# Weight loads of 1 MB instead of 512 KB in a decoder block on one Trainium2 core

## What is computed

```
h = rmsnorm(x, g_pre_mix)
nq, nkv, ngate, rq, rk, rv, rg, mq, bg = split(h @ w_in)            # 2048 x 12824
y_a = nsa_attention(nq, nkv, sigmoid(ngate), cmp_w1_k, cmp_w1_v, ...)  # 8 heads
y_b = retention(rq, rk, rv) * silu(rg)                              # 4 heads
y_c = memory_attention(mq, rmsnorm(mem) @ w_mem_kv)                 # 4 heads, 256 memory rows
merged = sum over 3 branches of sigmoid(bg[b]) * (y_b @ w_br[b])
x = x + rmsnorm(merged @ w_o, g_post_mix)
u = causal_dwconv(rmsnorm(x) @ w_up)                                # 2048 x 11264
x = x + rmsnorm((gelu(u_gate) * u_val) @ w_down, g_post_ffn)        # 5632 x 2048
```

## Time and profile before

| | us |
|---|---|
| median of 3 runs | 1735.86 (1735.41 to 1736.28) |
| the profiled execution, its own time | 1736.51 |
| span of that execution, first to last instruction | 1734.0 |
| mean granted TensorE clock | 0.998 of 2.4 GHz |
| PE busy | 1708.6 (99% of the span) |
| DVE, ACT, POOL busy | 1090.6, 817.0, 44.5 |
| moved by DMA | 327.77 MB, 189 GB/s in the mean |

### The profile page before, as it was taken

One profiled execution on the slowest core, in us unless ns is written; L12 is line 12 of the kernel. 1 busy time (PEld: TensorE's weight loads), 2 busy tenths in 40 slices (PEclk: granted clock), 3 DMA queues, 4 the chain that ended last, 5 costly groups with the idle time before them and its releaser, 6 DMA issues.

```text
span 1734.0 us, 26478 instructions
## 1 busy us (share of the span) xinstructions
PE 1708.6 (99%) x9645; PEld 1500.4 (87%) x9645; DVE 1090.6 (63%) x1430; ACT 817.0 (47%) x1111; POOL 44.5 (3%) x50
## 2 busy tenths in 40 slices
PE   6999999999999999999999999999999999999998
PEld 6998999999888888888888888888888888888886
DVE  5645557666566454564565667776676676676677
ACT  5533346444444434434444555454454454454453
POOL 0000000000041000000000000000000000000000
PEclk9999999999999999999999999999999999999999
DMA  8756467545555666666657555655666666656654
GB/s 262 223 184 188 146 194 243 161 131 165 157 189 180 193 196 193 214 197 193 190 179 241 184 171 190 189 192 187 189 194 189 188 193 189 192 187 191 191 184 141
DMA packets 246146, 327.77 MB, mean 189 GB/s; under 512 B 12727, under 2 KB 167464, under 8 KB 245544
## 3 DMA queue, kind: packets, MB, share of 16 engines
q1 hardware_dynamic: 246056, 326.47, 60.4%
HBM read 321.71 MB, written 3.67 MB: 188 GB/s over the span
## 4 chain that ended last, share of the span: by engine, by line
PE 94%; DVE 2%; DMA 2%; issue 1%; ACT 1%; SPq 0%; POOL 0%; POOLq 0%; DVEq 0%; ACTq 0%
PE bank L1347 18%; PE bank L1338 15%; PE bank L1337 15%; PE bank L1339 15%; PE bank L1351 9%; PE bank L1311 4%; PE bank L1313 4%; PE bank L1312 4%; PE bank L1324 1%; PE bank L1326 1%; PE bank L1325 1%; DMA wraw<-in_w_in 1%; DVE wlo L840 1%; PE bank L1647 0%; PE bank L1626 0%
## 5 line engine op out<-in xcount | busy, mean ns | idle before, releaser
L840 DVE TENSOR_TENSOR wlo<-wraw,whi 128x1024 fp32r<-128x1024 f32 x580 | 711.0, 1231 | 470.0 <-ACT whi L564 468.5
L564 ACT ACTIVATE whi<-wraw 128x1024 fp32r<-128x1024 f32 x580 | 613.2, 1060 | 702.0 <-PE bank L1339 390.5
L1347 PE MATMUL bank<-hx,whi 128*128 128x512 f32 x1376 | 344.5, 392 | 0.0
L1347 PEld LDWEIGHTS bank<-hx,whi 128*128 128x128 f32 x1376 | 248.0, 189 | 44.9
L1351 PEld LDWEIGHTS bank<-hx,wlo 128*128 128x128 f32 x1376 | 187.7, 190 | 13.4
L1351 PE MATMUL bank<-hx,wlo 128*128 128x256 f32 x1376 | 191.9, 282 | 0.0
L1337 PE MATMUL bank<-whi,hx 128*128 128x512 f32 x448 | 175.7, 392 | 0.0
L1339 PE MATMUL bank<-whi,hx 128*128 128x512 f32 x448 | 174.4, 389 | 0.0
L1338 PE MATMUL bank<-wlo,hx 128*128 128x512 f32 x448 | 174.3, 389 | 0.0
L1337 PE MATMUL bank<-whi,r_hi 128*128 128x512 f32 x384 | 149.8, 390 | 0.0
L1338 PE MATMUL bank<-wlo,r_hi 128*128 128x512 f32 x384 | 149.5, 389 | 0.0
(11 more groups left out here) (264 smaller groups left out, 2136.8 us busy)
## 6 DMA issues: line engine op xcount, KB each, us to landing
wraw<-in_w_in SPq DMA_DIRECT2D x200, 512.0 KB, 3.6
wraw<-in_w_up SPq DMA_DIRECT2D x176, 512.0 KB, 4.4
wraw<-in_w_down SPq DMA_DIRECT2D x88, 512.0 KB, 4.2
wraw<-in_w_mem_kv SPq DMA_DIRECT2D x32, 512.0 KB, 3.8
wraw<-in_w_o SPq DMA_DIRECT2D x32, 512.0 KB, 4.5
wraw<-in_w_br_mem SPq DMA_DIRECT2D x16, 512.0 KB, 4.3
wraw<-in_w_br_nsa SPq DMA_DIRECT2D x16, 512.0 KB, 4.5
wraw<-in_w_br_ret SPq DMA_DIRECT2D x16, 512.0 KB, 4.3
```

Source lines behind the costliest of these rows:

```text
L564: nc.scalar.activation(whi[:, c], wraw[:, c], ACT.Copy).then_inc(hi_done, 1)
L840: V.tensor_tensor(wlo[:, c], wraw[:, c], whi[:, c].bitcast(F32), ALU.subtract).then_inc(lo_done, 1)
L1347: T.matmul(ps[UP_PAIRS[j][t]][:, :], whi[:, c, k, t * P:(t + 1) * P], hx[:, :, k0 + k, :], start=first and k == 0, stop=False, skip_group_ ...
```

## The change

Two chunks come in one transfer and under one semaphore. A load waits until the second chunk of its pair of slots is free, then brings 1 MB; `loaded` has two semaphores instead of four, and `hi` of either chunk waits on its pair's. The number of loads through `wraw` falls from 588 to 294. The slots, the split, the matmuls and all program orders of ACT, DVE, POOL and PE stay as they are. The core of the diff:

```diff
-        loaded = [sem(f"loaded{c}") for c in range(4)]
+        loaded = [sem(f"loaded{h}") for h in range(2)]
...
-            def quad(q, src, dst=lambda c: wraw[:, c]):
-                for c in range(4):
+            def narrow_pair(h):
+                return wraw[:, 2 * h:2 * h + 2].rearrange("p c k n -> p (c k) n")
+            def wide_pair(h):
+                return wraw[:, 2 * h:2 * h + 2].rearrange("p c k n -> p (c k n)").rearrange("p (k n) -> p k n", n=2 * GW)
+            def quad(q, src, dst=narrow_pair):
+                for h in range(2):
                     if q:
-                        sp.wait_ge(lo_done, 4 * (q - 1) + c + 1)
-                    sp.dma_start(dst(c), src(c)).then_inc(loaded[c], 16)
+                        sp.wait_ge(lo_done, 4 * (q - 1) + 2 * h + 2)
+                    sp.dma_start(dst(h), src(h)).then_inc(loaded[h], 16)
...
             def loop(q0, trips, per, sources, ...):
-                    free = [sp.snap(4 * per * i + (4 * (q0 - 1) + k + 1)) for k in range(4 * per)]
+                    free = [sp.snap(4 * per * i + (4 * (q0 - 1) + 2 * k + 2)) for k in range(2 * per)]
...
-            quad(0, lambda c: rows(w_in, 4 * c, C_MQ))
+            quad(0, lambda h: rows(w_in, 8 * h, C_MQ, GW, 8))
...
-                return [lambda c, j=j: w[:, 2 * (c % 2):2 * (c % 2) + 2, (4 * j + 2 * (c // 2)) * GW:(4 * j + 2 * (c // 2) + 2) * GW]
-                        for j in range(2)]
+                return [lambda h, j=j: w[:, :, (4 * j + 2 * h) * GW:(4 * j + 2 * h + 2) * GW] for j in range(2)]
...
-                act.wait_ge(loaded[c], 16 * q + 16)
+                act.wait_ge(loaded[c // 2], 16 * q + 16)
```

More of the change, by code:

```diff
@@ L293, in _, with loop @@
         def _(sp):
[L294 to L296 removed]
+            def narrow_pair(h):
[4 more added lines that the diff above has]
+                for h in range(2):
                     if q:
[L299 to L302 removed]
+                        sp.wait_ge(lo_done, 4 * (q - 1) + 2 * h + 2)
+                    sp.dma_start(dst(h), src(h)).then_inc(loaded[h], 16)
+            def loop(q0, trips, per, sources, dst=lambda j, h: narrow_pair(h)):
                 with sp.Fori(0, trips) as i:
[L305 removed]
+                    free = [sp.snap(4 * per * i + (4 * (q0 - 1) + 2 * k + 2)) for k in range(2 * per)]
                     src = sources(i)
                     for j in range(per):
[L308 to L310 removed]
+                        for h in range(2):
+                            sp.wait_ge(lo_done, free[2 * j + h])
+                            sp.dma_start(dst(j, h), src[j](h)).then_inc(loaded[h], 16)
             def cols(w, base, count=2):
@@ L315, in sources @@
                     at = [sp.snap(count * GW * i + (base + GW * j)) for j in range(count)]
-                    return [lambda c, o=o: rows(w, 4 * c, o) for o in at]
+                    return [lambda h, o=o: rows(w, 8 * h, o, GW, 8) for o in at]
                 return sources
@@ L322, in sources, with into_wide @@
                     at = sp.snap(2 * GW * i + base)
-                    return [lambda c, j=j: rows(w, 8 * j + 2 * c, at, 2 * GW, 2) for j in range(2)]
+                    return [lambda h, j=j: rows(w, 8 * j + 4 * h, at, 2 * GW, 4) for j in range(2)]
                 return sources
-            def into_wide(j, c):
-                return wide(wraw, c)
+            def into_wide(j, h):
+                return wide_pair(h)
             def quarters(dst, src, sems):
@@ L351, in _ @@
             sp.dma_start(w2[:, 1], cmp_w2_v[0].rearrange("(k p) n -> p k n", p=P)).then_inc(s_pe2, 16)
-            quad(1, lambda c: rows(w_in, 4 * c, C_MQ + GW))
-            quad(2, lambda c: rows(w_in, 4 * c, C_MQ + 2 * GW))
+            quad(1, lambda h: rows(w_in, 8 * h, C_MQ + GW, GW, 8))
+            quad(2, lambda h: rows(w_in, 8 * h, C_MQ + 2 * GW, GW, 8))
             sp.wait_ge(s_rbc, 1)
@@ L358, in _ @@
                          arena[:, A_GATE:A_GATE + REL].unsqueeze(1).to_broadcast([P, P // COPIES, REL])).then_inc(s_scr, 16)
-            quad(3, lambda c: rows(w_in, 4 * c, C_MQ + 3 * GW))
+            quad(3, lambda h: rows(w_in, 8 * h, C_MQ + 3 * GW, GW, 8))
             sp.wait_ge(s_scr, 16)
@@ L366, in _ @@
             for n in range(3):
-                quad(Q0["kv0"] + n, lambda c: rows(w_in, 4 * c, C_KV + n * GW))
+                quad(Q0["kv0"] + n, lambda h: rows(w_in, 8 * h, C_KV + n * GW, GW, 8))
             sp.wait_ge(m_o, MH + 1)
@@ L374, in _ @@
                 if Q0["mix"] + m == CMP_LAST + 1:
[L376 to L379, removed]
+                    for h in range(2):
+                        sp.wait_ge(lo_done, 4 * (CMP_LAST - 1) + 2 * h + 2)
+                        sp.sem_inc(loaded[h], 16)
+                        sp.dma_start(narrow_pair(h), rows(w_in, 8 * h, C_KV + (3 + n) * GW, GW, 8)).then_inc(loaded[h], 16)
                     continue
                 if kind == "cmp":
-                    quad(Q0["mix"] + m, lambda c: rows((cmp_w1_k, cmp_w1_v)[n // 2], 16 * (n % 2) + 4 * c, 0))
+                    quad(Q0["mix"] + m, lambda h: rows((cmp_w1_k, cmp_w1_v)[n // 2], 16 * (n % 2) + 8 * h, 0, GW, 8))
                 else:
-                    quad(Q0["mix"] + m, lambda c: rows(w_in, 4 * c, C_KV + (3 + n) * GW))
+                    quad(Q0["mix"] + m, lambda h: rows(w_in, 8 * h, C_KV + (3 + n) * GW, GW, 8))
             loop(Q0["rqk"], 4, 2, cols(w_in, C_RQ))
@@ L406, in branch @@
                     at = [sp.snap(4 * GW * i + 2 * GW * j) for j in range(2)]
-                    return [lambda c, o=o: rows(w, 2 * c, o, 2 * GW, 2) for o in at]
+                    return [lambda h, o=o: rows(w, 4 * h, o, 2 * GW, 4) for o in at]
                 loop(Q0[f"br{n}"], 2, 2, branch, into_wide)
             for j in range(2):
-                quad(Q0["wo"] + j, lambda c: rows(w_o, 8 * j + 2 * c, 0, 2 * GW, 2), lambda c: wide(wraw, c))
+                quad(Q0["wo"] + j, lambda h: rows(w_o, 8 * j + 4 * h, 0, 2 * GW, 4), wide_pair)
             for j in range(2):
-                quad(Q0["wo"] + 2 + j, lambda c: rows(w_o, 8 * j + 2 * c, 2 * GW, 2 * GW, 2), lambda c: wide(wraw, c))
+                quad(Q0["wo"] + 2 + j, lambda h: rows(w_o, 8 * j + 4 * h, 2 * GW, 2 * GW, 4), wide_pair)
             sp.wait_ge(s_mgl, KT // 2)
@@ L423, in down, with step_dst @@
                 w = w_down[0, bass.ds(r0, 512), :].rearrange("(k p) n -> p k n", p=P)
-                return [lambda c, j=j: w[:, 2 * (c % 2):2 * (c % 2) + 2, (4 * j + 2 * (c // 2)) * GW:(4 * j + 2 * (c // 2) + 2) * GW]
-                        for j in range(2)]
-            def step_dst(j, c):
-                return wide(wraw, c) if j >= 4 else wraw[:, c]
+                return [lambda h, j=j: w[:, :, (4 * j + 2 * h) * GW:(4 * j + 2 * h + 2) * GW] for j in range(2)]
+            def step_dst(j, h):
+                return wide_pair(h) if j >= 4 else narrow_pair(h)
             for n in range(4):
-                quad(Q0["up0"] + n, lambda c: rows(w_up, 4 * c, up_col(n)))
+                quad(Q0["up0"] + n, lambda h: rows(w_up, 8 * h, up_col(n), GW, 8))
                 if n == 1:
@@ L439, in step @@
                 at = [sp.snap(512 * i + (512 + up_col(n))) for n in range(4)]
-                return [lambda c, o=o: rows(w_up, 4 * c, o) for o in at] + down(sp.snap(512 * i))
+                return [lambda h, o=o: rows(w_up, 8 * h, o, GW, 8) for o in at] + down(sp.snap(512 * i))
             loop(Q0["ffn"], STEPS - 1, 6, step, step_dst)
             for j in range(2):
-                quad(Q0["dn"] + j, down((STEPS - 1) * 512)[j], lambda c: wide(wraw, c))
+                quad(Q0["dn"] + j, down((STEPS - 1) * 512)[j], wide_pair)
             for n, (t, at, width) in enumerate(OUT_PARTS):
```

## The result

The changed kernel takes 1750.98 us in the median of 4 runs (1748.92 to 1751.54), the kernel before 1736.07 beside it: a ratio of 1.0085, 95% interval 1.0072 to 1.0098. It is slower by 14.9 us, forecast were 8.4. The profiled execution took 1751.54 (span 1749.2), 15.0 more than the one of before.

The account below looks back on a forecast made before the run. PE was taken as the bound, busy 1708.6 of 1734.0 us. Losses of 0.5 (quad 1), 1.4 (quad 3), 3.55 (mix), 1.2 (quad 81) and 1.7 (quad 147) made 8.4 us: 1744.3 us, range 1739.3 to 1750.0.

Parts of the forecast that it names:

- the middle of two cases: Quad 1: PE loses nothing if the pair lands early, 1.0 us if it lands with 1.1; 0.5 was taken.
- Mix, 3.55: Phase mix: PE's loss over three rounds of loads, up to 22.0, 3.55 us in all (2.95 to 6.55).
- X: Time from issue to landing of a 1 MB load: taken as 4.9 us, between 4.7 and 5.9.
- X - 2.3: Mix, at 20.0: PE's loss because the pair is requested later, 2.6 us.
- 3X - 11.15: Mix, up to 22.0: PE's loss after three rounds of loads, 3.55 us with the 2.6 at 20.0 inside.
- X - 3.2: Quad 147, at the end: PE's loss waiting for 147.2, 1.7 us (1.5 to 2.7).
- Start, 1.9: Quads 1 and 3: PE's loss from chunks landing together, 0.5 us in quad 1 and 1.4 in quad 3.
- 2X - 8.1: Behind quad 81: how much later ACT's row squares start; 0.5 us is covered, so PE loses 1.2 (0.8 to 3.2).
- What PE does next hangs on that chain: Behind quad 81: PE's next work depends on the delayed row squares and diagonal, so PE loses 1.2 us.
- A: Rival: 1 MB lands about as fast as 512 KB; 1737.7 us, not slower by 0.2%; chance 0.12.
- B: Rival: X near its upper bound because a pair shares the queue with its neighbour; sum 15.0, 1750.9 us; chance 0.12.
- C: Rival: PE's pause in mix drops its clock to 1.2 GHz, 4 us on top, 1748.3 us; chance 0.08.

Follow-up runs that it names:

- k_warm: Changed kernel plus matmuls that nobody reads in PE's two long pauses, before quad 20 and before 147.2; 1747.39 us, ratio 1.0071.
- k_fill: Changed kernel plus matmuls that nobody reads in three pauses, before quads 20 and 22 and before 147.2; 1752.58 us, ratio 1.0103.
- m_late: Kernel before, still 512 KB loads and four semaphores, but both loads of a pair wait for the second slot; 1739.18 us, ratio 1.002.
- w_start: k_warm with single 512 KB loads put back in quads 1 to 3; 1745.86 us, ratio 1.006.
- m_both: Kernel before, still 512 KB loads, but both loads of a pair wait for the second slot and share one semaphore; 1755.47 us, ratio 1.0116.
- w_wo: k_warm with single 512 KB loads put back in quads 75 to 82; 1747.66 us, ratio 1.0069.
- p_mix: Changed kernel with single 512 KB loads and their own semaphores put back in quads 20 to 23 and 25; 1742.63 us, ratio 1.0038.
- p_wo: Changed kernel with single 512 KB loads and their own semaphores put back in quads 75 to 82; 1750.37 us, ratio 1.0081.

## Why the prediction was wrong

The sign was right, and in the main the mechanism: PE waits in the short stages, and the feed-forward loop and the attention, gate and branch phases, put at nothing, cost nothing. The range ended at 1750.0, 1 us short. What failed are terms of the sum: mix left out the second pair of slots and the clock, the end left out the clock, the output projection left out quads 75 and 78 and put a chain at full price that gave most of it back, and quad 1 took the middle of two cases. The 6.8 us between 8.4 and 15.2 are these steps.

**Mix, 3.55 for 6.8.** The first part holds to a tenth: the pair was requested at 264.11, which is 261.54 and the 2.57 that PE was late by then, and PE's pause is X - 2.3 more than before (SP, ACT and PE):

```profile
264.11 3.50 SPq L308 DMA_DIRECT2D wraw<-in_w_in  x2
```

```profile
269.13 2.00 ACT L571 ACTIVATE whi<-wraw 128x1024 fp32r<-128x1024 f32 x2 [3.18 <-DMA wraw<-in_w_in]
...
284.91 1.06 ACT L571 ACTIVATE whi<-wraw 128x1024 fp32r<-128x1024 f32 x1 [1.79 <-PE bank L1333]
...
301.59 2.00 ACT L571 ACTIVATE whi<-wraw 128x1024 fp32r<-128x1024 f32 x2 [4.00 <-DMA wraw<-in_cmp_w_v]
```

```profile
271.59 0.35 PE L1331 MATMUL bank<-whi,hx 128*128 128x256 f32 x1 [2.96 <-DVE wlo L847]
...
303.96 0.39 PE L1616 MATMUL bank<-whi,r_lo 128*128 128x256 f32 x1 [1.24 <-DVE wlo L847]
```

Up to 22.0 the three rounds had 5.00, 5.47 and 4.99 us, so 3X - 11.15 becomes 4.3, and 4.1 was measured: the term stands, X was 0.25 too small a round (1.5 of the 4.1 are the half clock's at 20.0, and PE waited that much less for 22.0). What I left out is the other pair of each quad. 21.3 is converted only at 284.91, when PE lets its slot go, so 22.2/22.3 are requested at 287.26 and 23.2/23.3 at 296.18; their conversion at 301.59 holds PE up at 303.96 and again for the next chunk, with 0.4 more up to quad 25: 2.7 us. Part of these is the clock's too, since PE let that slot go later by it: in k_warm the same stretch cost 0.8. "Here three rounds of loads stand in a row" was true of one pair of slots; there are two, and they take turns.

**The end, 1.7 for 3.7.** X was 5.14, so the term X - 3.2 is 1.9 (1.81 of idle time), and the half clock behind it took 1.7 more. I had put the fall among the rivals, for mix alone and with a chance of 0.08. In mix, where I had priced it at 4 us, what it costs stays open between nothing and 3 us; at the end, where I had not looked for it, it counts in full.

**Start, 1.9 for 2.6.** For quad 1 I took the middle between two cases, and it was the later one: the first pair of quad 1 was converted at 29.98, 1.1 before at 30.06, and PE waited 1.2. Quad 3 gave 1.5 for 1.4.

**Output projection, 1.2 for 2.1.** The row squares began 1.8 us later against PE's work (990.95), nearly the 2X - 8.1 of the sum. PE idled 0.3 for the split of 81.2 in the pass before and 0.6 for the diagonal, but got 0.6 back at the next wait, which is shorter than before (PE after, then before):

```profile
982.95 0.50 PE L1373 MATMUL bank<-hx,m_hi 128*128 128x512 f32 x1 [0.29 <-DVE hx L844]
994.75 2.02 PE L1406 MATMUL bank<-work,arena 128*128 128x128 f32 x16 [0.58 <-issue]
997.40 0.36 PE L1389 MATMUL bank<-whi,hx 128*128 128x256 f32 x1 [0.63 <-DVE hx L1175]
```

```profile
985.93 0.36 PE L1382 MATMUL bank<-whi,hx 128*128 128x256 f32 x1 [1.34 <-DVE hx L1168]
```

So "What PE does next hangs on that chain" was wrong: in the kernel before, ACT came to that work only behind PE's last matmuls of quad 81. Of the staircase 0.6 stands before the row squares, at the split of 81.2, and 0.1 behind them. The rest is at quads 75 and 78 (0.3 and 1.05), for which the sum had no term: the first pair of 78 is requested beside the four loads of x and lands 11.7 us after its request (10.0 before). It is also the part that varies: 0.7 to 2.1 in the profiles of kernels with the same loads there (k_fill's new pause apart).

**X, 4.9 for 5.0 to 5.7.** It enters three of the five terms: mix, quad 81 and quad 147. Of my ways to it, 3.4 + 1.43 came nearest. The Trainium skill's 2.0 us plus bytes over 436 GB/s ("DMA: Bandwidth & Descriptors", anatomy) makes 4.4 of 1 MB; that section is on transfers that GpSimd issues, and these are issued by SP. The shortest landing of a pair here took 4.7, so for these loads the measurement decides.

**The rivals.** A falls with X. B gave 1750.9, nearly the time measured, by a mechanism that was not there: X stayed far from 5.9 in most places. C, the clock, was the one that I should have put into the sum. "TensorE: Matmul & The Clock Gate", Part 1, in the Trainium skill, has the clock fall when the array idles; the windows above, at 0.50 behind PE's pauses of 2.96 and 1.81 us, agree.

## What to carry to other kernels

Before making transfers larger, list for each stage how long a landed chunk lies before it is used, and compare that with the landing time plus what is now done to two chunks instead of one; here, where PE is the bound and the loads are hidden, larger transfers gained nothing, and they lost in the short stages, not in the long loop. Follow every slot of a ring separately, since each has its own chain of request, landing and release. And where a pause of 2 to 3 us appears on a TensorE that was never idle, price the half clock behind it, above all where no work follows (1.7 us here).

## What was not expected of the hardware

The clock's answer to a pause is not a function of the pause's length alone. Behind pauses of 2.7 us and more in the body it fell each time (to 1.2 GHz, for 3 to 7 us); behind 2.0 to 2.3 us it fell in m_late, w_start and at the end of m_both, not in k_warm and w_wo; behind 1.6 to 1.8 us at the end it fell in the changed kernel, not in p_mix and p_wo; and behind 1.25 and 0.52 us in a row at quad 23 it fell in m_both, not behind 1.24 and 0.52 at the same place in the changed kernel. That goes with runs of one kernel that differ by more than they did before, as m_late's two groups show. And two transfers of 512 KB requested one behind the other took 5.23 us for both to land, one of 1 MB 5.08. The second of the two requests left SP 0.56 us late, so this does not show that the larger transfer moves its bytes faster.
